# A two-layer encoder trunk on one core: mixer A's v made channel-major and turned, the gating bias added by VectorE

## The reference, cut to what matters

```python
h = rms_norm(x, mix_norm[l])
q, k, v, u, vg, cx, cb, cc, gl = split_columns(h @ w_in[l])   # k and v: 128 columns each
...
y_a = sliding_window_gqa(q, k, v, attn_sinks[l])              # uses v token by token
y_b = spatial_gating(gelu(u), gelu(vg), ...)                  # u * (w_s @ normed(vg) + b_s)
```

## Time and profile before

| | us |
|---|---|
| three timed runs | 1589.98, 1590.48, 1591.97 (median 1590.48) |
| the profiled execution, its own time | 1589.14 |
| its span in the trace | 1587.3 |
| PE busy | 1314.4 (83%) |
| DVE busy | 598.0 (38%) |
| ACT busy | 447.4 (28%) |
| the chain that ended last | PE 53%, DMA 36%, DVE 6% |

### The profile page before, as it was taken

One profiled execution on the slowest core, in us unless ns is written; L12 is line 12 of the kernel. 1 busy time (PEld: TensorE's weight loads), 2 busy tenths in 40 slices (PEclk: granted clock), 3 DMA queues, 4 the chain that ended last, 5 costly groups with the idle time before them and its releaser, 6 DMA issues.

```text
span 1587.3 us, 31259 instructions
## 1 busy us (share of the span) xinstructions
PE 1314.4 (83%) x13623; PEld 1020.7 (64%) x13623; DVE 598.0 (38%) x987; ACT 447.4 (28%) x665; POOL 0.4 (0%) x5
## 2 busy tenths in 40 slices
PE   9999999998777586877679999999986656767755
PEld 8999999995354263544448999999754323324422
DVE  5869647644121101212118885566431101101101
ACT  7544545532120110102016454554301001000101
POOL 0000000000000000000000000000000000000000
PEclk9999999999889788999979999999999988878988
DMA  9843458449999999999997544664799999999996
GB/s 356 294 162 107 160 188 315 147 169 392 416 427 420 427 426 422 427 420 426 427 387 233 198 149 160 242 251 148 281 417 429 425 428 424 427 428 414 427 427 281
DMA packets 93839, 520.02 MB, mean 328 GB/s; under 512 B 9850, under 2 KB 17410, under 8 KB 68356
## 3 DMA queue, kind: packets, MB, share of 16 engines
q1 hardware_dynamic: 92956, 515.94, 81.1%
q10 hardware_dynamic: 744, 2.05, 0.4%
HBM read 515.87 MB, written 2.10 MB: 326 GB/s over the span
## 4 chain that ended last, share of the span: by engine, by line
PE 53%; DMA 36%; DVE 6%; ACT 2%; issue 2%; SPq 2%; DVEq 0%; ACTq 0%
DMA ring<-in_w_expert_out 29%; PE banks L1759 29%; PE banks L2202 6%; PE banks L2155 5%; DMA ring<-in_w_expert_in 4%; PE banks L1790 4%; PE banks L2216 2%; DMA ring<-in_w_in 2%; PE banks L2172 2%; DVE w_lo L1066 1%; DVE stat L1520 1%; PE banks L1988 1%; SPq L514 1%; ACT w_hi L647 1%; DMA lnt<-in_positions 1%
## 5 line engine op out<-in xcount | busy, mean ns | idle before, releaser
L2155 PE MATMUL banks<-ring,arena 128*32 128x256 f32 x3904 | 267.1, 423 | 123.0 <-DMA ring<-in_w_expert_in 117.3
L2155 PEld LDWEIGHTS banks<-ring,arena 128*32 128x32 f32 x3904 | 125.9, 119 | 247.3 <-DMA ring<-in_w_expert_in 147.4
L1066 DVE TENSOR_TENSOR w_lo<-ring,w_hi 128x2048 fp32r<-128x2048 f32 (+1 forms) x103 | 210.5, 2044 | 108.9 <-ACTq L624 97.1
L1759 PE MATMUL banks<-h_hi,w_hi 128*128 128x256 f32 x776 | 221.8, 286 | 0.9 <-DVEq L1057 0.9
L2202 PE MATMUL banks<-ring,arena 128*32 128x256 f32 x2048 | 154.2, 451 | 81.8 <-DMA ring<-in_w_expert_out 68.6
L1759 PE MATMUL banks<-h_hi,w_lo 128*128 128x256 f32 x776 | 219.5, 283 | 0.0
L1002 ACT ACTIVATE arena<-banks 128x128 f32<-128x128 f32 x66 | 18.4, 278 | 689.1 <-PE banks L2155 689.1
L1513 DVE TENSOR_TENSOR arena<-arena,banks 128x128 f32<-128x128 f32 x66 | 19.1, 289 | 504.2 <-ACT arena L1002 504.2
L1759 PE MATMUL banks<-h_lo,w_hi 128*128 128x256 f32 x712 | 201.4, 283 | 0.0
L647 ACT CAST w_hi<-ring 128x2048 fp32r<-128x2048 f32 (+1 forms) x103 | 176.1, 1709 | 70.0 <-PE banks L1759 43.0
L2202 PEld LDWEIGHTS banks<-ring,arena 128*32 128x32 f32 x2048 | 76.2, 125 | 137.4 <-issue 79.4
(11 more groups left out here) (434 smaller groups left out, 2179.9 us busy)
## 6 DMA issues: line engine op xcount, KB each, us to landing
ring<-in_w_expert_in SPq DMA_DIRECT2D x120, 2048.0 KB, 23.3
ring<-in_w_expert_out SPq DMA_DIRECT2D x60, 2048.0 KB, 24.1
ring<-in_w_in SPq DMA_DIRECT2D x23, 2048.0 KB, 9.2
ring<-in_w_branch SPq DMA_DIRECT2D x12, 1024.0 KB, 5.2
ring<-in_w_out SPq DMA_DIRECT2D x4, 2048.0 KB, 7.9
ring<-in_w_xq SPq DMA_DIRECT2D x4, 2048.0 KB, 7.9
ring<-in_w_xo SPq DMA_DIRECT2D x4, 2048.0 KB, 8.4
arena<-in_w_xkv SPq DMA_DIRECT2D x4, 2048.0 KB, 21.3
```

Of the source, the lines that this page charges most:

```text
L1066: post(dve.tensor_tensor(piece_view(w_lo, *key), piece_view(ring, *key), high_view(*key).bitcast(F32), ALU.subtract), "w_split")
L1759: ins = pe.matmul(acc, stationary(a, k), moving(b, k), start=k == 0 and n == 0, stop=k == kc - 1 and n == 2)
L2155: ins = pe.matmul(G[32 * j:32 * j + 32, :], tokens, w[:, k % 4, :, j * P:(j + 1) * P], start=k == 0, stop=k == KC - 1, tile_position=(0, 3 ...
```

## The change

Five edits. In the table of jobs a job `vt` is inserted between u and rot. v is computed as k is: the weights' own 128 columns are the stationary operand and the 256 tokens the moving one, so that it comes out by channel; ACT copies it to `vT`, PE turns it in two 128x128 transposes (`vt`), just before the rotations, and ACT copies the turned blocks to `vtok` (in layer 1 scaled by the norm's factor). These copies move from before u's read-out to after it. The bias row is loaded on all 128 partitions; PE's two bias matmuls and its wait for that load go; DVE adds the bias to the bank before it multiplies.

```diff
-MIX_JOBS = ([("q", 2), ("k", 1), ("v", 1), ("u", 2), ("rot", 4), ("vg", 2), ("ws", 1), ("s", 4),
+MIX_JOBS = ([("q", 2), ("k", 1), ("v", 1), ("u", 2), ("vt", 1), ("rot", 4), ("vg", 2), ("ws", 1), ("s", 4),
...
-        bs = sb("bs", [1, 512])
+        bs = sb("bs", [P, 512])
...
+        vT = kraw[:, 1, :]
...
-                sp.dma_start(bs[0:1, :], A["gmlp_b_s"][layer].rearrange("g i -> (g i)").unsqueeze(0)).then_inc(S["ln_loaded"], 16)
+                sp.dma_start(bs[:, :], A["gmlp_b_s"][layer].rearrange("g i -> (g i)").unsqueeze(0).broadcast_to([P, 512])).then_inc(S["ln_loaded"], 16)
...
                 evac(layer, "k", 0, kraw[:, 0, :], "qraw_ready", view=lambda a: a[:, 0:T])
+                evac(layer, "v", 0, vT, "qraw_ready", view=lambda a: a[:, 0:T])
...
+                turned = lambda a: a[:, 0:T].rearrange("p (t c) -> p t c", t=TB)
+                if layer:
+                    acc = turned(job_wait(act, layer, "vt"))
+                    for tb in range(TB):
+                        link(act.activation(vtok[:, tb, :], acc[:, tb, :], ACT.Copy, scale=mix_rstd_tok[:, tb:tb + 1]))
+                    act.sem_inc(free(layer, "vt"), 1)
+                    act.sem_inc(S["v_ready"], 1)
+                else:
+                    evac(layer, "vt", 0, vtok[:, 0:2, :], "v_ready", view=turned)
+                post(act.copy(vtok[0:64, 2, :], vtok[0:64, 1, :]), "v_ready")
+                post(act.copy(vtok[64:P, 2, :], vtok[64:P, 0, :]), "v_ready")
...
                     acc = job_wait(dve, layer, "mixed", tb)
+                    link(dve.tensor_tensor(acc, acc, bs[:, :], ALU.add))
...
                 acc = job_begin(pe, layer, "v")
-                for tb in range(TB):
-
-                    ins = three(acc[:, tb * T:(tb + 1) * T], w, x, KC, lambda a, k: x[a][:, k, tb * P:(tb + 1) * P],
-                                lambda b, k: w[b][:, k, :])
-                done(ins)
+                done(three(acc[:, 0:T], w, x, KC, lambda a, k: w[a][:, k, P:2 * P], lambda b, k: x[b][:, k, :]))
...
-                pe.wait_ge(S["qraw_ready"], 3 * layer + 3)
+                pe.wait_ge(S["qraw_ready"], 4 * layer + 4)
+                acc = job_begin(pe, layer, "vt")
+                for tb in range(TB):
+                    ins = pe.transpose(acc[:, tb * P:(tb + 1) * P], vT[:, tb * P:(tb + 1) * P], ident)
+                done(ins)
...
-                pe.wait_ge(S["ln_loaded"], 48 * (layer + 1))
                 for tb in range(TB):
                     acc = job_begin(pe, layer, "mixed", tb)
-                    pe.matmul(acc, ones[0:1, :], bs[0:1, :], start=True, stop=False, skip_group_check=True)
                     for g in range(4):
-                        ins = pe.matmul(acc[:, g * P:(g + 1) * P], vg[:, tb, g * P:(g + 1) * P], wsT[:, g, :],
-                                        start=False, stop=g == 3, skip_group_check=True)
+                        ins = pe.matmul(acc[:, g * P:(g + 1) * P], vg[:, tb, g * P:(g + 1) * P], wsT[:, g, :], start=True, stop=True)
```

More of the change, by code:

```diff
@@ L825, in _ @@
                     act.sem_inc(free(layer, "rtok"), 1)
-                    acc = job_wait(act, layer, "v").rearrange("p (t c) -> p t c", t=2)
-                    for tb in range(TB):
[L828 to L834, removed]
                 for i in range(2):
@@ L1238, in _ @@
                     dve.sem_inc(free(layer, "rot", i), 1)
-                    dve.wait_ge(S["qraw_ready"], 3 * layer + i + 1)
+                    dve.wait_ge(S["qraw_ready"], 4 * layer + i + 1)
                     if i < 2:
```

## The result

The changed kernel takes 1604.37 us (median of 4 runs, 1602.72 to 1606.31), the kernel before 1590.23 beside it (1589.56 to 1591.97): 1.0087 times as long, 95% interval 1.0075 to 1.0099. The forecast was 1603.4. The profiled execution took 1603.72 against 1589.14, so 14.6 us are to be explained, where the prediction had 12.9.

What follows compares the result with a forecast made beforehand. Loads bound the experts, PE the mixers. Waits +8.3 us and clock 4.6 gave +12.9 on the profiled 1589.14, so 1602.0; that execution lay 1.34 below the median, hence 1603.4 us, range 1596.5 to 1608.

Steps and rivals of the forecast that it cites:

- v and vt: v's 24 matmuls instead of 48 save 2.88 us in layer 0, nothing in layer 1; vt costs 0.22 per layer.
- The turn: vt's two transposes on PE's path before the rotations: 0.22 us per layer, 0.44 if as dear as four.
- The addition: Each of DVE's two bias additions of 128x512 takes 0.69 us, upper end 1.4; with steps 1.46 us per layer.
- br00 waits for DVE: DVE has no gap before br00's split, so br00 starts later: +1.4 us in layer 0, +1.5 in layer 1.
- The bank of xo,0: Shifted banks put xo,0 behind xpv,1, so xo's first steps wait for `o_part(1)`: 3.9 us per layer.
- The waits' sum: All terms without the clock: +2.6 us in layer 0, +5.6 in layer 1, together +8.3 (rounded).
- The clock: Granted clock falls after PE's four idle stretches: 1.7 us each at xo, 0.6 each at br00, 4.6 together.
- the second rival: Clock falls in all four stalls at full 2.2 us, and in layer 1's u: about 1608.5 us; chance 0.08.
- The stream of loads: PE's gain or loss in a mixer before xo's end moves the expert loads and the end by the same amount.

## Why the prediction was right, and where not

- **v and vt, right.** br00 of layer 0 starts 1.27 us earlier; the prediction's terms give -2.88 + 0.22 + 1.4 = -1.3. It did not say why a gain on PE should pass through a place that DVE sets; the trace does (DVE's queue begins that much sooner). The chain has v, k and u as 144 matmuls in 17.28 us where there were 168 in 20.16. In layer 1 nothing came, as predicted: PE waits 3.5 us in three pieces for low parts of u, 1.90, 0.89 and 0.69, where it waited 0.23 and 0.69 before. v alone gained 1.9 us.
- **The turn** costs 0.22 us, two transposes at 90.22 and the rotations at 90.44, as the rows had it.
- **The addition, right.** 0.70 us each, with source and result in a bank; 0.69 was taken from the earlier trace rows. By the Trainium skill ("VectorE: DVE Perf Modes", section "The TRN2 errata"), which sets 120 cycles of fixed cost against 58, each would be about 0.07 us dearer than from SBUF, an estimate; the trace does not bear that out here: 699 ns beside 693 for the product of the same size that has both operands in SBUF (L1205, L1201 before).
- **br00 waits for DVE, right.** 3.77 and 3.76 us of idle time, 3.5 and 3.9 predicted. In layer 1 the delay from u,1 to br00 is 1.4 us where 0.22 + 1.5 stood. vt's 0.22 is in it (the kernel with the bias alone, which has no vt, is delayed by 1.14), so it is the additions that cost 1.1 there and not 1.5: DVE's queue in layer 1 had, before the change, an idle time of 0.66 us near its start where the other passes have 0.31.
- **The bank of xo,0, right, and the largest term.** 3.9 us of waiting per layer were predicted and 3.93 measured (3.89 with the fillers), and the shift alone costs 11.9 with its clock.
- **The waits' sum** was 8.3 predicted, 7.9 measured.
- **The clock, mis-sized.** The step "I take 1.7 each, for br00 0.6 each: 4.6 us" (1.7 for each stall at xo) came out as 1.5, 2.6, 1.3 and 2.6, together 8.0. The mechanism was as stated, though the forecast took the fall for some of the stalls only: all four were followed by one. Two of the four lasted twice as long as the others, behind stalls of the same length. The bound of 2.2 for one stall, from the 24 matmuls of the earlier trace rows, was too low: 2.6 was reached twice. The Trainium skill ("TensorE: Matmul & The Clock Gate", section "HAM oscillation — how this bites in real kernels") tells of waits between bursts that each throw the clock back; the trace agrees, four times of four, which was most of the second rival's condition (its fall in layer 1's u did not come). That rival lost because it had the full 2.2 for each of them, 8.8, and another 1 for u.
- **The stream of loads, nearly right.** That what PE loses "moves the whole stream, and the end, by the same amount" came out as 15.9 us of loss for 14.6 of end: the expert stages gave back 0.4 and 0.9. This error and that of the clock have opposite signs, which is why the total came out closer than its terms: 8.3 + 4.6 against 7.9 + 8.0 - 1.3. The nearness of 1603.4 to 1604.37 is in this part luck.
- **Two slips in reading**, without effect on the sum: slice 10, counted to the expert stages, has 392 GB/s and not 414 or more, and the 22nd slice has 233, the 198 stands in the 23rd.

Left open: why the lower level lasted some 3.4 us in some cases and 6.8 in others. It is not the layer or the length of the stall: behind the stall before br00 it lasted 3.4 us in both layers of the kernel with the bias alone, 6.8 in both with vt outside the order, 6.8 and 3.4 with `o_part(1)` sooner, 3.4 and 6.8 in the changed kernel. Also open is which instructions in the expert stages took up the 1.3 us.

## What to carry to other kernels

A table that gives resources out in turn (banks, buffers, slots) makes every new entry a change for all entries behind it: look up the new predecessor of each job, and when it is released, before counting instructions; here that was over four fifths of the cost. Work moved from a busy engine to an idle-looking one (38% busy) costs its full length where that engine's queue has no gap just there, and here the stall that it opened was paid a second time in clock. Where PE must wait some microseconds, matmuls without use ahead of the wait bought back 6.4 of 14 us.

## What was not expected of the hardware

- The granted clock fell with no stall at all. Kernel with PE's bias and the moved splits, layer 0: PE is busy through both windows (1.50 of 1.50, 3.50 of 3.50), and the clock goes from 1.00 to 0.54; no idle time of PE stands in the 30 us before. The chain of waits shows what runs there, pv, then the one-row bias matmuls (L1959) and the products of 128 columns (L1961):

```profile
149.00:150.50 1.50, 1.50 (x9) 1.15 (x10) 1.06 (x3) 0.76 (x1) 0.00 (x0) 1.00 1.05 411
150.50:154.00 3.50, 3.50 (x15) 2.80 (x14) 2.76 (x5) 0.00 (x0) 0.00 (x0) 0.54 0.04 10
```
```profile
146.01 1.90 PE banks L1951 x32
147.91 1.05 PE banks L1959 x2
148.96 1.09 PE banks L1961 x8
150.05 1.22 PE banks L1959 x2
151.28 2.01 PE banks L1961 x8
```

  The same products (four, in eight records) take 1.09 us and then 2.01. Such a fall at this place, some 14 us ahead of br00, is in four of the ten passes through a mixer that were profiled with PE's bias matmuls, and in none of the fourteen without them. That the one-row matmuls bring it about was not tested; if they do, their removal has this small merit on the other side of the ledger.
- A wait of 1.9 us was followed by a fall in some executions (v alone: 0.50 from 854 to 861 us in layer 1) and by none in others (the splits moved: waits of 1.85 and 1.84 us in layer 1, 1.00 throughout). The stalls of 3.7 us and more were followed by one in every profile that had them, except where fillers stood in them.
